# Four picks of one unit moved into the value pass, late row operations spread evenly, and key one-hots made on GpSimd

## The reference, cut to what matters

```
q = (xt @ w_q).reshape(n, 8, 2, 128)                 # 8 heads, two half keys
s = einsum("nhpd,hpkd->nhpk", q, sub_keys)           # 128 keys per half
s1, i1 = top_k(s[:, :, 0], 16); s2, i2 = top_k(s[:, :, 1], 16)
top_s, pos = top_k(s1[..., :, None] + s2[..., None, :], 16)
experts = i1 * 128 + i2 at pos                       # 16 picks of 16384 experts
g = softmax(top_s)
a = gelu(einsum("td,thkd->thk", x, u_tab[experts]))
out = einsum("thk,thkd->td", g * a, v_tab[experts])
```

## Time and profile before

| what | before |
|---|---|
| median of 3 runs | 2037.63 us (2035.4 to 2044.22) |
| the profiled execution, its own time | 2045.1 us |
| its span, first to last instruction | 2043.8 us |
| granted TensorE clock, mean | 0.939 of full speed |
| busy share of the span: PE, DVE, ACT, POOL | 88%, 73%, 45%, 31% |
| bytes moved, mean rate | 627.88 MB, 307 GB/s |

### The profile page before, as it was taken

One profiled execution on the slowest core, in us unless ns is written; L12 is line 12 of the kernel. 1 busy time (PEld: TensorE's weight loads), 2 busy tenths in 40 slices (PEclk: granted clock), 3 DMA queues, 4 the chain that ended last, 5 costly groups with the idle time before them and its releaser, 6 DMA issues.

```text
span 2043.8 us, 28687 instructions
## 1 busy us (share of the span) xinstructions
PE 1800.4 (88%) x11068; PEld 1601.6 (78%) x11068; DVE 1497.3 (73%) x1987; ACT 925.4 (45%) x1474; POOL 630.8 (31%) x549
## 2 busy tenths in 40 slices
PE   6999999999999999957765353699999999999997
PEld 6999999999999887746764243578878888888886
DVE  4464444444465548988889899878878889998997
ACT  5444444444444441223433999644333343343433
POOL 0000000001044003477777677112211114454430
PEclk9999999999999999978998555899999999999999
DMA  9555555555466869999999999498999999999994
GB/s 310 167 170 168 166 167 174 174 165 167 144 185 219 316 242 419 364 402 410 410 406 412 372 409 396 165 346 343 396 387 374 398 376 375 396 404 399 403 400 193
DMA packets 293543, 627.88 MB, mean 307 GB/s; under 512 B 10364, under 2 KB 223405, under 8 KB 234958
## 3 DMA queue, kind: packets, MB, share of 16 engines
q0 software_dynamic: 48400, 343.95, 41.8%
q1 hardware_dynamic: 244558, 282.20, 40.4%
q10 hardware_dynamic: 496, 0.58, 0.1%
HBM read 622.45 MB, written 8.44 MB: 309 GB/s over the span
## 4 chain that ended last, share of the span: by engine, by line
PE 72%; DVE 9%; ACT 8%; DMA 5%; POOL 3%; DVEq 2%; issue 1%; SPq 0%; ACTq 0%; POOLq 0%
PE ps L2010 34%; PE ps L1671 27%; DVE u_ring L1494 4%; PE ps L1838 4%; PE ps L1852 3%; DMA u_ring<-in_peer_u,idx_all 3%; DVEq L1444 2%; ACT ones L1131 2%; ACT ones L1140 1%; ACT ones L1137 1%; POOL u_ring L707 1%; ACT u_ring L1072 1%; POOL u_ring L698 1%; DMA raw<-in_w_out 1%; DMA v_raw<-in_peer_v 1%
## 5 line engine op out<-in xcount | busy, mean ns | idle before, releaser
L1253 DVE TENSOR_TENSOR w_lo<-raw,w_hi 128x2048 fp32r<-128x2048 f32 x112 | 259.0, 2313 | 324.5 <-ACT w_hi L780 324.5
L1671 PE MATMUL ps<-act_hi,w_hi 128*128 128x256 f32 x1536 | 442.1, 288 | 4.6 <-DVE act_lo L1377 2.9
L1671 PE MATMUL ps<-act_lo,w_hi 128*128 128x256 f32 x1536 | 435.9, 284 | 0.0
L1671 PE MATMUL ps<-act_hi,w_lo 128*128 128x256 f32 x1536 | 435.8, 284 | 0.0
L1188 ACT ACTIVATE v_hi<-v_raw 128x2048 fp32r<-128x2048 f32 x128 | 245.5, 1918 | 405.7 <-PE ps L2010 205.8
L2010 PE MATMUL ps<-v_hi,c_hi 128*128 128x512 f32 x1024 | 403.9, 394 | 4.3 <-DVE c_lo L1569 4.3
L2010 PE MATMUL ps<-v_hi,c_lo 128*128 128x512 f32 x1024 | 403.6, 394 | 0.0
L2010 PE MATMUL ps<-v_lo,c_hi 128*128 128x512 f32 x1024 | 402.6, 393 | 0.0
L1565 DVE TENSOR_TENSOR v_lo<-v_raw,v_hi 128x2048 fp32r<-128x2048 f32 x128 | 293.2, 2291 | 73.9 <-ACT v_hi L1188 73.4
L1494 DVE CUSTOM_DVE_ANT_0 u_ring<-u_ring,ps 128x2048 f32<-128x2048 f32 x144 | 326.3, 2277 | 23.0 <-DMA u_ring<-in_peer_u,idx_all 22.6
L780 ACT ACTIVATE w_hi<-raw 128x2048 fp32r<-128x2048 f32 x112 | 214.1, 1911 | 262.8 <-PE ps L1671 217.5
(11 more groups left out here) (246 smaller groups left out, 2258.9 us busy)
## 6 DMA issues: line engine op xcount, KB each, us to landing
v_raw<-in_peer_v SPq DMA_DIRECT2D x128, 1024.0 KB, 7.3
raw<-in_w_in SPq DMA_DIRECT2D x80, 1024.0 KB
raw<-in_w_out SPq DMA_DIRECT2D x16, 1024.0 KB
wq<-in_peer_w_q SPq DMA_DIRECT2D x8, 2048.0 KB, 13.8
raw<-in_w_br_a SPq DMA_DIRECT2D x16, 512.0 KB
bias_by_query<-bias_by_distance POOLq DMA_DIRECT2D x1, 4096.0 KB, 21.2
bias_st<-bias_by_query POOLq DMA_DIRECT2D x16, 256.0 KB, 4.5
raw<-in_w_br_b SPq DMA_DIRECT2D x16, 256.0 KB
```

Source lines behind the costliest of these rows:

```text
L1253: nc.vector.tensor_tensor(w_lo[:, j % NHL], raw[:, j % NRAW], w_hi[:, j % NHL].bitcast(F32), ALU.subtract).then_inc(lo_done, 1)
L1671: last = nc.tensor.matmul(out_ap, w_parts[wp][:, slot, k], act_parts[ap][:, k], start=(k == k0 and m == 0), stop=(k == k1 - 1 and m == 2))
```

## The change

There are three edits.

1. The last four picks of unit 11 (k = 12 to 15, `MOVED = 4`) leave `EARLY`, so 188 rows are dotted in the pick stage. They become late operations: `LATE` now has 68 picks, dotted as n = 0 to 67 and added as n = 68 to 135. Unit 11's weights are made in two parts (`COEF_PARTS`); the softmax numerators of the four are kept aside and their places in `cw_all` set to zero (`late_picks_kept`), so that tile 2's matrices leave them out.
2. `OPS_AT` deals the operations from n = 12 on evenly over blocks 17 to 124, instead of one a block with an extra one in every ninth or so of the second half.
3. The `pre` one-hots are made by GpSimd, four `tensor_scalar` with `is_equal` a group, between the gathers of n = 156 to 185 (`KEYS_AT`), instead of by ScalarE in unit 11. ScalarE takes 23 of tile 1's groups instead of 21, VectorE 9 instead of 11.

```
-DVE_GROUP_AT = {at: n for n, at in enumerate([(9, k) for k in (1, 5, 9, 14)] + [(10, k) for k in (1, 5, 9, 14)] + [(11, k) for k in (1, 5, 9)])}
+DVE_GROUP_AT = {at: n for n, at in enumerate([(9, k) for k in (3, 8, 13)] + [(10, k) for k in (3, 8, 13)] + [(11, k) for k in (1, 3, 6)])}
+KEYS_AT = {156 + 8 * g // 3: g for g in range(N_PRE)}
+MOVED = 4
+LATE = [(N_EARLY - 1, k) for k in range(PTOP - MOVED, PTOP)] + [(u, k) for u in range(N_EARLY, NU) for k in range(PTOP)]
-LATE_OPS = N_LATE * PTOP
+LATE_OPS = len(LATE)
-    b = n + n // 3 if n < 12 else n + 4 - max(n - LATE_OPS, 0) // 10
+    b = n + n // 3 if n < 12 else 17 + (n - 12) * 108 // (2 * LATE_OPS - 12)
-EARLY = [(u, k) for u in range(N_EARLY) for k in range(PTOP)]
+EARLY = [(u, k) for u in range(N_EARLY) for k in range(PTOP) if (u, k) not in LATE]
...
+        def key_ones(g):
+            if g == 0:
+                pool.wait_ge(kt_ev, 1)
+            for m in range(GTOK):
+                last = nc.gpsimd.tensor_scalar(pre[g // 4][:, g % 4, m], iota_f[:, :], pick2[:, 1, GTOK * g + m:GTOK * g + m + 1], None, ALU.is_equal)
+            last.then_inc(pre_ok, 1)
...
+            if n in KEYS_AT:
+                key_ones(KEYS_AT[n])
...
-        def key_ones(g):
-            rows = pre[g // 4][:, g % 4]
-            for m in range(GTOK):
-                last = nc.scalar.activation(rows[:, m], iota_f[:, :], ACT.Abs, scale=-1.0, bias=pick2[:, 1, GTOK * g + m:GTOK * g + m + 1])
-            last.then_inc(ka_ok, 1)
-            act.wait_ge(ka_ok, g + 1)
-            nc.scalar.activation(rows, rows, ACT.Relu, scale=-1.0, bias=one_col[:, :]).then_inc(pre_ok, 1)
...
+        def late_picks_kept():
+            w = cw_all[:, PTOP * N_EARLY - MOVED:PTOP * N_EARLY]
+            dve.wait_ge(ex_ok, N_EARLY)
+            nc.vector.tensor_copy(exp_late[:, :], w)
+            dve.drain()
+            nc.vector.memset(w, 0.0)
...
+        late_picks_kept()
         gelu_argument(N_EARLY - 1)
         coefficients(N_EARLY - 1)
```

More of the change, by code:

```diff
@@ L101 @@
 LATE_GROUPS = PTOP * (N_EARLY - PH) // GTOK
-LATE_OPS = N_LATE * PTOP
+MOVED = 4
+LATE = [(N_EARLY - 1, k) for k in range(PTOP - MOVED, PTOP)] + [(u, k) for u in range(N_EARLY, NU) for k in range(PTOP)]
+LATE_OPS = len(LATE)
+COEF_PARTS = ([(u, 0, PTOP) for u in range(N_EARLY - 1)] + [(N_EARLY - 1, 0, PTOP - MOVED), (N_EARLY - 1, PTOP - MOVED, PTOP)]
+              + [(u, 0, PTOP) for u in range(N_EARLY, NU)])
+LATE_PART = {MOVED + PTOP * m - 1: N_EARLY + m for m in range(N_LATE + 1)}
 V_FEW = 16
@@ L318, in build @@
     late_dots = at("late_dots", 203.125, [P, 2, PTOP])
-    dots = [early_dots[:, u] if u < N_EARLY else late_dots[:, u % 2] for u in range(NU)]
+    part_dots = [(early_dots[:, u] if n < N_EARLY else late_dots[:, u % 2])[:, k0:k1] for n, (u, k0, k1) in enumerate(COEF_PARTS)]
+    exp_late = at("exp_late", 203.0625, [P, MOVED])
     gel = at("gel", 203.25, [P, 2, PTOP])
@@ L1175, in _ @@
                 dve_group_out(DVE_GROUP_AT[c, k] - 1)
-            if c == N_EARLY - 1 and 2 <= k < 2 + N_PRE:
-                key_ones(k - 2)
         matrices(ACT_GROUPS - 1)
@@ L1214, in _ @@
             for n in OPS_AT[b - 1] if b else ():
[L1215 to L1217 removed]
+                if n in LATE_PART:
+                    squared(LATE_PART[n])
+                    tanh_of(LATE_PART[n])
         nc.scalar.activation(one_root[:, :], one_col[:, :], ACT.Sqrt)
@@ L1494, in dot @@
             nc.vector.tensor_tensor_reduce(out=u_ring[:, slot], in0=u_ring[:, slot], in1=h2p[u // PH], scale=0.5, scalar=0.0,
-                                           op0=ALU.mult, op1=ALU.add, accum_out=dots[u][:, k:k + 1]).then_inc(dot_ok, 1)
+                                           op0=ALU.mult, op1=ALU.add, accum_out=early_dots[:, u, k:k + 1]).then_inc(dot_ok, 1)
         def diagonal(u, k):
@@ L1549, in _ @@
                 gelu_argument(c - 1)
-            if c > 0 and k == (13 if c <= 2 else 1 if c == PH else 12):
+            if c > 0 and k == (13 if c <= 2 else 1 if c == PH else 10 if c == N_EARLY - 1 else 12):
                 coefficients(c - 1)
@@ L1586, in late_op @@
                 nc.vector.tensor_tensor_reduce(out=row_ring[slot][:, :], in0=row_ring[slot][:, :], in1=xg[:, 1], scale=0.5, scalar=0.0,
-                                               op0=ALU.mult, op1=ALU.add, accum_out=dots[unit][:, k:k + 1]).then_inc(dot_ok, 1)
+                                               op0=ALU.mult, op1=ALU.add, accum_out=late_dots[:, unit % 2, k:k + 1]).then_inc(dot_ok, 1)
                 return
```

61 lines of the change are left out of this document (29 added, 32 removed).

## The result

The changed kernel takes 2059.28 us (median of 4 runs, 2058.29 to 2059.77). The kernel before took 2039.39 us beside it (4 runs, 2035.40 to 2044.22). The ratio is 1.0099, 95% interval 1.0082 to 1.0116: slower by 20 us. The forecast was 2033 us, with 0.13 for slower.

A forecast was written before the change was run, and what follows sets the result against it. ScalarE and VectorE were taken to bound the pick stage, TensorE the value pass. The terms -11.5 + 4 + 2 + 1 = -4.5 us, from the median 2037.6, gave 2033 us, range 2024 to 2043.

The forecast's parts named there:

- Work must leave both to shorten this stage: End of pick stage, 1150 to 1286: ScalarE (133.86 us busy of 136) and VectorE (128.26) are both full.
- I take 1.2, since the operation has one tensor input: GpSimd, pick stage: a key block of four operations costs 1.2 us (1.13 to 1.8), twelve 14.4 us.
- Gather 187 comes some 3 us later: GpSimd, pick stage: 11.3 us of room for 14.4 of key blocks; 5 us of gather delay cost nothing.
- Rival D: GpSimd becomes the bound: port collisions make a key block 4.2 us, +32 us, 2070; decides from 2.4 us a block; chance 0.11.
- Two groups fewer are worth 3.6 to 5.4 us: VectorE, pick stage: nine one-hot groups instead of eleven save 4.5 us, before new collisions.
- The new collisions with key blocks, 3 us: VectorE, pick stage: seven groups fall among GpSimd's key blocks; collisions cost 3 us (0 to 8).
- the 14 us worked out from it: Pick stage, by the skill's port rule: all twelve key blocks paid in full at 1.2 us, leaving no gain.
- Four dots go: VectorE, pick stage: four dots of 2.28 us leave, saving 9.1 us.
- The value pass, +7: Value pass: first-half double blocks 4 us (eight stalls of about 0.5), residual 2, late blocks of second half 1.
- The residual's stall: Value pass, block 36: fuller queue lengthens TensorE's wait of 3.5 us by 2 us (0 to 4).
- rival C: Transfers bound the second half: 410 GB/s asked against about 402 lengthens 64 blocks by 2%, 7 us; total 2040; chance 0.17.
- the forecast of 11.5: Pick stage ends 11.5 us earlier: VectorE's balance -10.2 us, plus 1.3 from ScalarE's smaller lag.

The follow-up runs named there:

- the square: Four kernels: key one-hots on ScalarE or late on GpSimd, four picks in pick stage or pass; ratios to the kernel before 1, 1.0001, 1.0002, 0.9941.
- all remedies: Changed kernel with key blocks after the last gather, two-operation blocks in second half, residual loads apart: 2039.39 us, 0.9993; VectorE's groups moved too: 2029.67 us, 0.9939.

## Why the prediction was wrong

**What bounds the kernel: right.** "Work must leave both to shorten this stage" is what the square shows. What was missed is that a third engine must have room where the work is put, not only in sum.

**"I take 1.2, since the operation has one tensor input": the step that failed first.** Ten of the twelve blocks measured 2.35 to 2.37 us and two 2.56 and 2.80, all above the upper bound of 1.8 too. The bounds came from a selection at 283 ns and a two-input addition at 452 ns; an operation with a scalar of its own for each partition, which no row of before had, costs 616. The price isn't contention: ten blocks agree within 0.02 us, after the last gather the 48 are no cheaper (30.68 us), and in the run with the groups moved and all remedies seven of them took 626 ns each from 1265.9 to 1269.2, while VectorE stood idle. The Trainium skill (GPSIMD Engine Reference, 4.1 Engine selection) calls GpSimd "roughly line-rate" for one input and some two times slower than VectorE for two. For two inputs the trace agrees: 1276 ns over 128x512 against VectorE's 0.68 us. For one it does not: 616 ns over 128x128 against about 0.28 us, and more than GpSimd's own 452 ns for two inputs over as many elements.

**"Gather 187 comes some 3 us later": failed with it.** It came 20.1 us later. The prediction's own balance, 12 x 2.36 - 11.3 - 5, gives 12.0 us in place of -1.9, and taking the blocks away from between the gathers gave back 13.1 us. Rival D named the place, the balance and the deciding price, 2.4 us a block, and the measured price stands at it; its sum would have been 2037.6 + 12.0 - 9 + 7 = 2048. Its cause, VectorE taking the ports from the key blocks, was not it. (Such a loss exists, but is small: in that run with the groups moved, 13 operations beside VectorE's one-hots of tile 2, from 1272.8 to 1280, took 770 ns each.) D had 0.11 because the price was tied to contention instead of left open for an operation never seen.

**"Two groups fewer are worth 3.6 to 5.4 us", less 3 for collisions: failed.** The groups cost 1.6 us more, not 1.5 less. I costed the groups as a number and took the new places as equal. `DVE_GROUP_AT` puts six of them after dots 3, 8 and 13, where GpSimd's products begin. In the changed kernel the late gathers hide part of this, since VectorE waits anyway; with the gathers on time it is 38.3 against 20.6 us, and 0.9993 against 0.9939. The harm goes on from there, as GpSimd's wait for dots shows (19.0 against 5.5 us). A warning stood in the earlier trace rows: the group after dot 1 of unit 11 was undisturbed, the one after dot 9 met a pair of multiplications. That such a thing follows from the place was not asked.

**The new collisions with key blocks, 3 us: wrong in kind.** A key block is four instructions of 0.6 us each. The two groups of the changed kernel that met only a key block, by their own durations:

```profile
1231.95 0.97 DVE L1544 TENSOR_TENSOR ones_d<-iota_f,pickT 128x512 f32<-128x512 f32 x1
1232.85 1.23 DVE L1538 TENSOR_SCALAR ones_d<-iota_f,pickT 128x128 f32<-128x128 f32 x4
...
1247.05 0.69 DVE L1544 TENSOR_TENSOR ones_d<-iota_f,pickT 128x512 f32<-128x512 f32 x1
1247.65 1.37 DVE L1538 TENSOR_SCALAR ones_d<-iota_f,pickT 128x128 f32<-128x128 f32 x4
```

They took 2.2 and 2.06 us, 0.4 and 0.3 above the 1.8, while a pair of multiplications that begins inside half a group costs it 2.6 to 3.0 us. By the Trainium skill (SBUF — State Buffer, 🔬 SBUF: two separate sides) the loser waits for the winner's whole instruction. The trace fits that loosely: a pair is two instructions of 1.25 us and the group paid for both, a key block is four of 0.6 us and the group paid for less than one. So the 14 us worked out from it were far too much. Why the two kinds differ is shown by no run.

**"Four dots go", -9.1 us: right, on a condition.** Shown by the square: the stage goes from 124.3 to 116.9, 7.4 us, when ScalarE is relieved as well, and stays at 124.8 when it is not.

**The value pass, +7: right in its mechanism, somewhat small.** Seven waits of 0.5 us, 3.6 in all, stand for the forecast eight, 4 us; the eighth double block, 37, comes right behind the residual's stall and adds no wait of its own. An example from the chain; its eight lines are the order of work that was forecast: `v_hi` at the block boundary, `v_lo` of the block before, two late dots, the next remainders.

```profile
1412.76 1.92 ACT v_hi L1193
...
1414.70 2.29 DVE v_lo L1580
1417.00 0.34 DVE c_lo L1584
1417.33 2.20 DVE row_ring L1601
...
1419.54 2.20 DVE row_ring L1601
...
1421.75 2.20 DVE v_lo L1580
1423.96 0.35 DVE c_lo L1584
...
1424.35 22.59 PE ps L2025 x96
```

The residual's stall rose from 3.5 to 6.4 us, +2.9 for a forecast of +2. The second half held: window 1700 to 2010,

```profile
1700.00:2010.00 310.00, 310.00 (x1351) 253.41 (x1352) 297.29 (x181) 126.65 (x115) 156.62 (x65) 1.00 1.00 408
```

408 GB/s for a forecast of 410, with TensorE never waiting, so rival C falls. The first half and the residual make 3.6 + 2.9 = 6.5 of the 8.9 us. Tile 2's matrices, from the transposition to the pass, took 0.9 us more (1328.28 - 1295.15 = 33.1 against 1321.59 - 1289.38 = 32.2); the other 1.5 us are not placed. The dip of the clock at the residual stands in both traces.

**The sum.** The forecast was 26.3 us off. By the traces the stage ended 5.8 us later, not 11.5 earlier: 17.3 us. The pass was 1.9 off. The median of before is now 2039.4, not 2037.6: 1.8. The other 5 us are the difference between the gap of the two traces, 14.7, and that of the medians, 20; no trace here places them. With both failed steps repaired, the blocks late and the groups moved, the stage is 124.8 - 111.7 = 13.1 us shorter than before, so the forecast of 11.5 was sound for engines that have room.

## What to carry to other kernels

Before work moves to a third engine, take the price of that very operation there from a run or leave its upper bound wide, and ask in which stretch the engine is idle: 29 us of blocks between gathers cost 13 us, and with 31 us of the same blocks after the last gather nobody waited for them. When two engines are both nearly full, an edit that relieves one shows no gain; judge such edits in pairs. A table of places is a cost of its own: the same nine groups took 38 or 21 us by which dot they followed, so lay each place beside the other engine's timeline first. And before two traces are compared at one point, look at a point ahead of every edit: here it moved by up to 8.8 us, more than most of the effects.
